# Conv taps spread over more of attention, a latent projection that starts on half its input, and two smaller moves in a decoder trunk kernel on one Trainium2 core

## The chip, the core and the metric

One core of a Trainium2 chip (trn2). The time is the device time of one execution in microseconds. A core has TensorE (PE, matrix products and transposes), VectorE (DVE), ScalarE (ACT), GpSimd (POOL), SyncE (SP, which here only issues DMA transfers), and 16 DMA engines. Each engine works its own instructions in order and waits for others by semaphores.

## What is computed

Two layers of a decoder trunk over 1024 tokens of width 1024, all in float32. Cut to what matters:

```python
for i in range(2):
    a = rmsnorm(h, mix_norm_g[i])
    z = a @ w_in[i]                       # 1024 x 1440: 512 SGU | 512 conv | 416 latent (MLA)
    z_sgu, z_conv, c_q, c_kv, k_pe = split(z)
    y_a = sgu_mixer(z_sgu, ...)
    y_b = conv_mixer(z_conv, ...)         # a * sigmoid(g), causal depthwise conv of 31 taps, layernorm, silu, 256 x 256
    y_c = mla_mixer(c_q, c_kv, k_pe, ...) # 8 heads, causal softmax attention, q and k of width 96, v of width 64
    h = h + concat(rmsnorm(y_a), rmsnorm(y_b), rmsnorm(y_c)) @ w_o[i]
    m = rmsnorm(h, ffn_norm_g[i])
    h = h + hier_moe(m, ...)              # top 2 of 32 experts
    gate = sigmoid(rmsnorm(h, ple_norm_g[i]) @ ple_gate_w[i])
    e = rmsnorm(p[i] @ ple_proj_w[i], ple_post_norm_g[i])
    h = h + gate * e
```

## The kernel before

The 1024 tokens are 8 tiles of 128 rows. `h` stays on the chip. Every engine has its own program, and all loop over the two layers. A layer has five stages, and the order of the work inside each is written by hand, as a list of (lag, function) pairs for each engine that `lag_loop` works off: an entry (2, f) handles tile t + 2 in step t, an entry (-3, f) tile t - 3. Steps before tile 0 and after tile 7 are written out, so a tile index is a plain integer there. `settle` counts up a semaphore that nobody waits for. `turned`, `turn` and the rest wait on `Steps`, which are semaphores with counted, named events.

1. **Projections.** For each tile: ScalarE squares `h`, GpSimd takes the inverse root, VectorE scales (`norm(0)`, factors in `gains[:, MIX]`), TensorE transposes 8 blocks (`turn(0)`, line 1708), ScalarE copies them out of PSUM in two halves (lines 902 and 905, events `FX.lo` and `FX.hi`: blocks 0 to 3 and 4 to 7 of the contraction), and TensorE multiplies by `w_in` in three products of 8 steps each through the helper `product` (line 1739): `z_mla` (416 columns), `z_first` and `z_glu` (512 each). One step of a float32 product is two matmul instructions in the profile, so a product is x16. In the list of TensorE, `z_mla` of tile t + 1 stands behind the transposes of the queries of tile t - 2 (`r_turn`, line 1858) and ahead of everything of tile t. Its wait for both halves is in `turned(0, t)`. The q and k of each tile are stored to DRAM and loaded back head by head by SyncE.
2. **The conv on VectorE.** `taps(t, u, some)` (lines 1218 to 1223) works 256 columns (two tiles) of one half of the channels: tap k is one multiply-add of 128x256 into one of two accumulators, and after the last of the 31 taps line 1229 joins the two. There are 8 such jobs in a layer, numbered as the tiles. In the projection stage they run with a lag of 3, cut in three parts (taps 0 to 7, 8 to 18, 19 to 30), between the other VectorE work. Job 5 falls to the steps behind tile 7, where only it, the last gated half (line 1251) and the last `sgu_out` are left. Jobs 6 and 7 are done in attention: two taps behind the other VectorE work of each block j >= 4.
3. **Attention.** Head by head, and in a head block by block (j = 0 to 7: query tile j against key tiles 0 to j). TensorE: scores of the next block (lines 1896, 1899), transposes of this one (1910), output of the last one (1926). VectorE: row maximum of the next block (1393), copy of up to four transposed blocks (1399), output scaling of the last (1404, 1406), then taps. ScalarE: exponential (1017) and the other transposed blocks (1011). The program is unrolled.
4. **Output product, router and experts.** `w_o` product (`w_half`), `norm_m` with the factors in `gains[:, FFN]`, router, expert blocks. An expert block of 64 rows leaves its result in `y_half`, which is `gains[:, FFN, 0:512]`. The stage of the experts streams weights from DRAM.
5. **Gate.** For each tile VectorE adds the expert results (lines 1652, 1655), `norm(2)` scales by `ple_norm_g` (in `gains[:, MIX]`), TensorE transposes (`turn(2)`) and multiplies by the gate weights in two halves of 8 steps (`ple_main`: g_lo, g_hi), ScalarE takes the tanh of each half, VectorE gates and adds. The list of TensorE is (1, transposes), (0, both halves). The next layer's `mix_norm_g` overwrites `gains[:, MIX]`, so SyncE loads it behind all of the gate stage's norms.

## Time and profile before

| what | us |
|---|---|
| median of 3 runs (lowest, highest) | 2265.92 (2262.76, 2273.8) |
| the profiled execution, whole | 2260.44 |
| its span | 2258.3 |
| busy: TensorE, VectorE, ScalarE, GpSimd | 2032.6 (90%), 1097.2 (49%), 576.5 (26%), 377.6 (17%) |

The span runs from the first to the last recorded instruction; the whole is 2.1 us longer. Layer 0 fills about the first half of the span, layer 1 the second: the projections run from 0 to 281 us and from 1146 to 1408 us, attention behind them to 471 and 1598 us. A row of a timeline gives the start in us, the duration in us, the engine and line, the operation with its tiles and shape, how many instructions are merged (x), and in brackets the idle time in front of it on that engine with what ended it.

### The profile page before, as it was taken

To read this page: it belongs to the slowest core of one execution; us is meant where nothing else is said; L and a number is where in the kernel's file an instruction comes from. 1 tells how busy PE (TensorE), PEld (TensorE's weight loads), DVE (VectorE), ACT (ScalarE), POOL (GpSimd) and SP (SyncE) were. 2 spreads that over 40 slices of the span, in tenths; PEclk is the share of its full clock that TensorE was granted. 3 is DMA by queue.
4 is the path that set the end of the run, shared out by engine and by line. 5 is a ranking of instruction groups with operands and counts; after the bars stand their busy time and mean duration, and the time that the engine had idled before them with its cause. 6 is when DMAs were issued, how large, how long until landed. Compare 5 with 4: busy or idle time off the path is not lost.

```text
span 2258.3 us, 34453 instructions
## 1 busy us (share of the span) xinstructions
PE 2032.6 (90%) x8968; PEld 1167.5 (52%) x8968; DVE 1097.2 (49%) x2503; ACT 576.5 (26%) x1329; POOL 377.6 (17%) x550
## 2 busy tenths in 40 slices
PE   4999789999979999968979997999999799999698
PEld 2555467755545444434435554777555454444344
DVE  2479978855341111115424799788552411111353
ACT  2333234322131111111123332344221311111111
POOL 1222200012012222210012222000120122222100
PEclk9999889999989999988989998899999899999799
DMA  6011141000179999955310111410002799999422
GB/s 242 15 28 28 40 151 43 15 10 29 70 296 363 382 381 380 381 222 212 113 28 15 28 28 50 141 43 15 10 28 82 290 374 388 382 377 382 169 84 93
DMA packets 122170, 361.93 MB, mean 160 GB/s; under 512 B 18805, under 2 KB 53957, under 8 KB 105172
## 3 DMA queue, kind: packets, MB, share of 16 engines
q1 hardware_dynamic: 104980, 318.74, 38.6%
q0 software_dynamic: 14784, 33.59, 3.9%
q10 hardware_dynamic: 2304, 8.39, 1.0%
q8 instruction: 46, 0.75, 0.1%
q14 instruction: 56, 0.46, 0.1%
HBM read 319.50 MB, written 59.51 MB: 168 GB/s over the span
## 4 chain that ended last, share of the span: by engine, by line
PE 65%; DMA 15%; DVE 8%; issue 8%; ACT 1%; SPq 1%; POOLq 1%; POOL 1%; DVEq 0%; ACTq 0%
PE ps L1739 33%; DMA region_a<-moe_inputs,idx_ring 8%; PE ps L1896 5%; PE ps L2096 4%; PE ps L1926 4%; DMA region_c<-in_moe_w_up_dram 3%; PE ps L2075 3%; PE ps L1708 3%; PE ps L1910 2%; PE ps L2071 2%; PE ps L1828 2%; DMA region_a<-in_moe_w_up_dram 2%; PE ps L2056 2%; DMA h<-in_x_dram 1%; PE ps L1996 1%
## 5 line engine op out<-in xcount | busy, mean ns | idle before, releaser
L1739 PE MATMUL ps<-region_b,region_c 128*128 128x512 f32 x1024 | 452.8, 598 | 2.7 <-DVE region_c L1202 2.7
L1739 PE MATMUL ps<-region_a,region_c 128*128 128x512 f32 (+1 forms) x768 | 320.9, 572 | 14.9 <-ACT region_c L905 14.9
L1739 PEld LDWEIGHTS ps<-region_b,region_c 128*128 128x128 f32 x1024 | 194.0, 192 | 229.6 <-issue 229.1
L1739 PEld LDWEIGHTS ps<-region_a,region_c 128*128 128x128 f32 x768 | 145.4, 192 | 172.9 <-issue 172.9
L1619 DVE SCALAR_TENSOR_TENSOR region_a<-region_a,ps 128x128 f32<-128x128 f32 x66 | 23.4, 355 | 368.6 <-ACT region_a L1080 364.7
L1896 PE MATMUL ps<-region_c 96*128 96x512 f32 (+3 forms) x384 | 157.9, 522 | 0.0
L2075 PE MATMUL ps<-region_c,region_a 128*128 128x512 f32 x336 | 148.3, 594 | 8.2 <-DMA region_c<-in_moe_w_up_dram 8.1
L1926 PE MATMUL ps<-region_c,region_a 128*128 128x64 f32 x1152 | 148.0, 275 | 0.0
L1926 PEld LDWEIGHTS ps<-region_c,region_a 128*128 128x128 f32 x1152 | 144.5, 198 | 0.0
L1708 PE MATMUL ps<-ident,region_c 128*128 128x128 f32 x496 | 71.1, 293 | 77.1 <-DVE region_c L1186 59.6
L1017 ACT ACTIVATE region_a<-ps,neg_max 128x128 f32<-128x128 f32 (+7 forms) x128 | 94.9, 741 | 126.7 <-DVE neg_max L1393 125.2
L1393 DVE TENSOR_REDUCE neg_max<-ps 128x1 f32<-128x128 f32 (+7 forms) x128 | 96.5, 755 | 43.0 <-PE ps L1899 42.3
L1708 PEld LDWEIGHTS ps<-ident,region_c 128*128 128x128 f32 x496 | 62.6, 151 | 102.5 <-DVE region_c L1186 74.0
L1080 ACT ACTIVATE region_a<-ps 128x128 f32<-128x128 f32 x66 | 21.8, 331 | 346.1 <-PE ps L2075 233.2
L1910 PE MATMUL ps<-ident,region_a 128*128 128x128 f32 x576 | 88.3, 281 | 22.1 <-ACT region_a L1017 22.1
L2075 PEld LDWEIGHTS ps<-region_c,region_a 128*128 128x128 f32 x336 | 62.2, 190 | 86.5 <-issue 86.5
L2056 PE MATMUL ps<-ident,region_a 128*128 128x128 f32 (+1 forms) x528 | 59.6, 256 | 38.8 <-DMA region_a<-moe_inputs,idx_ring 19.6
L1910 PEld LDWEIGHTS ps<-ident,region_a 128*128 128x128 f32 x576 | 63.2, 144 | 52.2 <-ACT region_a L1017 35.2
L2071 PE MATMUL ps<-region_c,region_a 128*64 128x256 f32 x736 | 88.2, 394 | 1.3 <-DVE region_a L1613 1.2
L2075 PE MATMUL ps<-region_a 128*128 128x512 f32 x192 | 84.7, 594 | 4.0 <-DMA region_a<-in_moe_w_up_dram 2.7
L2056 PEld LDWEIGHTS ps<-ident,region_a 128*128 128x128 f32 (+1 forms) x528 | 47.9, 142 | 77.4 <-issue 77.4
L1896 PEld LDWEIGHTS ps<-region_c 96*128 96x128 f32 x384 | 66.6, 200 | 32.2 <-issue 31.7
(341 smaller groups left out, 2955.0 us busy)
## 6 DMA issues: line engine op xcount, KB each, us to landing
region_c<-in_moe_w_gate_dram SPq DMA_DIRECT2D x44, 1024.0 KB
region_c<-in_moe_w_up_dram SPq DMA_DIRECT2D x44, 1024.0 KB
region_c<-in_moe_w_down_dram SPq DMA_DIRECT2D x44, 1024.0 KB
region_a<-in_moe_w_gate_dram SPq DMA_DIRECT2D x22, 1024.0 KB
region_a<-in_moe_w_up_dram SPq DMA_DIRECT2D x22, 1024.0 KB
region_a<-in_moe_w_down_dram SPq DMA_DIRECT2D x22, 1024.0 KB
region_c<-choice_outputs SPq DMA_DIRECT2D x32, 512.0 KB, 4.4
qk_heads<-gains SPq DMA_DIRECT2D x32, 384.0 KB, 4.2
```

The costliest lines, as they stand in the source:

```text
L1017: nc.scalar.activation(prob[j % 2][:, 0:n], banks(2 * (j % 2))[:, 0:n], ACT.Exp, bias=neg_max[:, j % 2:j % 2 + 1], accum_out=denom[:, j:j ...
L1393: v.tensor_reduce(neg_max[:, j % 2:j % 2 + 1], banks(2 * (j % 2))[:, 0:(j + 1) * P], AX.X, ALU.max, negate=True).then_inc(*X_max.next(f"ma ...
L1708: ins = T(bank(b + k // 4, P * (k % 4), P * (k % 4) + P), src[:, P * k:P * k + P], ident[:, :])
L1739: ins = mm(dst, lhsT[:, k, :], w[:, k, a:b], start=(k == 0), stop=(k == KD - 1))
L1828: ins = mm(bank(half, 0, w), cnT[:, k, :], w_uq[:, k, w * half:w * half + w], start=(k == 0), stop=(k == 1))
L1896: mm(bank(b + c // 512, 0, w), q, k_ring[u][0:QK, c:c + w], start=True, stop=not last, skip_group_check=True)
L1910: ins = T(bank(4 + k // 4, P * (k % 4), P * (k % 4) + P), prob[j % 2][:, P * k:P * k + P], ident[:, :])
L1926: ins = mm(bank(6 + j % 2, 0, HEAD), prob_t[j % 2][:, k, :], vals[:, k, head, :], start=(k == 0), stop=(k == j))
L2056: ins = T(bank(k // 4, w * (k % 4), w * (k % 4) + w), x_blk[s][0:w, P * k:P * k + P], ident[0:w, 0:w])
L2071: ins = mm(ps[a:a + HALF, 2, 0:F].rearrange("p (a f) -> p a f", a=2), xT[:, k, 0:HALF], pair[:, :, P * c:P * c + P], start=(k == 0), stop= ...
L2075: ins = mm(bank(2).rearrange("p (a f) -> p a f", a=2), xT[:, k, :], w_gu[s][:, :, k, :], start=(k == 0), stop=(k == KD - 1))
L2096: ins = mm(bank(4 + half), hid_t[:, k, :], w_dn[s][:, k, 512 * half:512 * half + 512], start=(k == 0), stop=(k == 1))
```

## The change

Four edits.

- **Taps.** Job 5 of the conv leaves the steps behind tile 7 of the projection stage. Attention now works jobs 5, 6 and 7, 93 taps in place of 62: one tap behind the VectorE work of each block j < 4, two behind each block j >= 4, so 12 in a head, from head 0 on.
- **Latent projection.** `z_mla` no longer goes through `turned` and `product`. It waits for the first four transposed blocks, multiplies them, then waits for the other four and multiplies those. Its other waits come first.
- **Gate stage.** The list of TensorE becomes: first half of tile t, transposes of tile t + 1, second half of tile t.
- **Norm factors.** `ple_norm_g` goes to `gains[:, FFN]`, and the next layer's `mix_norm_g` is loaded to `gains[:, MIX]` right behind it, ahead of the expert weights, and not at the end of the layer. The 64-row expert results go to `junk[:, 0:512]`.

```diff
-        y_half = gains[:, FFN, 0:512]
+        y_half = junk[:, 0:512]
...
                 sp.dma_start(gains[:, BRANCH], I["ple_post_norm_g"][l].partition_broadcast(P)).then_inc(ple_loaded, 16)
-                sp.dma_start(gains[:, MIX], I["ple_norm_g"][l].partition_broadcast(P)).then_inc(ple_loaded, 16)
+                sp.wait_ge(*FM.a.before(TILES * l + TILES))
+                settle(sp, passed)
+                sp.dma_start(gains[:, FFN], I["ple_norm_g"][l].partition_broadcast(P)).then_inc(ple_loaded, 16)
+
+                def next_mix():
+                    load_mix((l + 1).with_bounds(max_val=DEPTH - 1))
+
+                guarded(sp, l < DEPTH - 1, next_mix)
...
-                def next_mix():
-                    sp.wait_ge(*FX.a.before(24 * l + 24))
-                    settle(sp, passed)
-                    load_mix((l + 1).with_bounds(max_val=DEPTH - 1))
-
-                guarded(sp, l < DEPTH - 1, next_mix)
...
-                                                         gains[:, BRANCH if ph == 1 else MIX, a:b], ALU.mult, ALU.mult)
+                                                         gains[:, (MIX, BRANCH, FFN)[ph], a:b], ALU.mult, ALU.mult)
...
-                        if not (isinstance(t, int) and t >= TILES - 2):
+                        if not (isinstance(t, int) and t >= TILES - 3):
                             taps(t, u, range(a, b))
...
-                    if j >= 4:
-
-                        some = range(8 * (hd % 4) + 2 * (j - 4), min(8 * (hd % 4) + 2 * (j - 4) + 2, TAPS))
-                        taps(TILES - 2 + hd // 4, hd // 4, some, acc_last)
+                    first = 12 * hd + j + max(j - 4, 0)
+                    for k in range(first, min(first + 1 + (j >= 4), 3 * TAPS)):
+                        taps(TILES - 3 + k // TAPS, (1 + k // TAPS) % 2, [k % TAPS], acc_last)
...
                 def z_mla(t, u, i):
                     g = TILES * l + t
-                    turned(0, t)
                     pe.wait_ge(*ZM_act.after(g - 1))
                     pe.wait_ge(w_in_loaded[2], 16 * l + 16)
-                    product(bank(4, 0, MLA_IN), aT_mix[u], w_in, 1024, IN).then_inc(*ZM_pe.next("z_mla"))
+                    settle(pe, passed)
+
+                    for steps_, some in ((FX.lo, range(0, 4)), (FX.hi, range(4, KD))):
+                        pe.wait_ge(*steps_.after(24 * l + t))
+                        settle(pe, passed)
+                        for k in some:
+                            ins = mm(bank(4, 0, MLA_IN), aT_mix[u][:, k, :], w_in[:, k, 1024:IN], start=(k == 0), stop=(k == KD - 1))
+                    ins.then_inc(*ZM_pe.next("z_mla"))
...
-                def ple_main(t, u, i):
-                    g = TILES * l + t
-                    turned(2, t)
-                    for k, half in enumerate(("g_lo", "g_hi")):
+                def ple_half(k):
+                    def go(t, u, i):
+                        g = TILES * l + t
+                        if k == 0:
+                            turned(2, t)
                         pe.wait_ge(*E_act.after(g - 1, ("t_lo", "t_hi")[k]))
-                        product(bank(2 + k), aT[u], ple_g, 512 * k, 512 * k + 512).then_inc(*E_pe.next(half))
-
-                lag_loop(pe, [(1, turn(2)), (0, ple_main)])
+                        product(bank(2 + k), aT[u], ple_g, 512 * k, 512 * k + 512).then_inc(*E_pe.next(("g_lo", "g_hi")[k]))
+                    return go
+
+                lag_loop(pe, [(0, ple_half(0)), (1, turn(2)), (0, ple_half(1))])
```

How the rows of the program move, at three places. **TensorE, in the loop of the projection stage, from the query transposes to the latent projection.** In brackets stand the semaphores that a row waits for: `x_lo` and `x_hi` are the two copied halves, `zm_act` the copy of the last latent result. Before:

```order
L1858 MATMUL ps<-ident,region_b 96x128 x7
L394 UNCONDITIONAL_BRANCH
L1734 ISA
L1753 ISA [waits x_hi,x_lo]
L1739 MATMUL ps<-region_a,region_c 128x416 [waits w_in_loaded2,zm_act]
L1739 MATMUL ps<-region_a,region_c 128x416 x7
```

Now:

```order
L1863 MATMUL ps<-ident,region_b 96x128 x7
L394 UNCONDITIONAL_BRANCH
L1751 ISA
L1756 ISA [waits zm_act,w_in_loaded2]
L1759 MATMUL ps<-region_a,region_c 128x416 [waits x_lo]
L1759 MATMUL ps<-region_a,region_c 128x416 x3
L1759 MATMUL ps<-region_a,region_c 128x416 [waits x_hi]
L1759 MATMUL ps<-region_a,region_c 128x416 x3
```

The wait for the second half has moved from two rows ahead of the product into its middle, and the first matmul itself now waits for the first half alone.

**VectorE, from the last join of the projection stage into head 0 of attention.** Before:

```order
L1229 TENSOR_TENSOR conv_in<-region_b,region_c 128x256
L1392 ISA
L1393 TENSOR_REDUCE neg_max<-ps 128x1
L1392 REGISTER_ALU
L1393 TENSOR_REDUCE neg_max<-ps 128x1
L1398 ISA
L1399 COPY region_a<-ps 128x128
L1392 REGISTER_ALU
L1393 TENSOR_REDUCE neg_max<-ps 128x1
```

Now:

```order
L1309 TENSOR_TENSOR region_c<-region_b 128x256
L1392 ISA
L1393 TENSOR_REDUCE neg_max<-ps 128x1
L1392 REGISTER_ALU
L1393 TENSOR_REDUCE neg_max<-ps 128x1
L1398 ISA
L1399 COPY region_a<-ps 128x128
L1216 ISA
L1217 ISA
L1218 TENSOR_SCALAR region_b<-conv_in,conv_w_cols 128x256
L1392 REGISTER_ALU
L1393 TENSOR_REDUCE neg_max<-ps 128x1
```

The first row maximum follows `sgu_out` at once, the 31 taps and the join in front of it are gone, and the first of them stands between the second and the third row maximum.

**TensorE, the loop of the gate stage.** Before:

```order
L1708 MATMUL ps<-ident,region_c 128x128 x8
L1734 ISA
L2128 ISA
L1739 MATMUL ps<-region_b,region_c 128x512 x8
L2128 REGISTER_ALU
L1739 MATMUL ps<-region_b,region_c 128x512 x8
```

Now:

```order
L2134 ISA
L1738 MATMUL ps<-region_b,region_c 128x512 x8
L1714 ISA
L1720 REGISTER_ALU
L1707 MATMUL ps<-ident,region_c 128x128 x8
L2134 REGISTER_ALU
L1738 MATMUL ps<-region_b,region_c 128x512 x8
```

The eight transposes have gone from ahead of the first half to between the halves; the number of instructions is the same.

## Rows read from the trace of the kernel before

**Rows 1.** Busy us (x) of PE, PEld, DVE, ACT, POOL, clock: projections.

```profile
189.50:218.20 28.70, 27.95 (x99) 15.33 (x98) 25.88 (x65) 9.82 (x25) 7.60 (x6) 1.00 0.11 27
...
274.00:288.00 14.00, 5.89 (x25) 4.52 (x25) 13.68 (x36) 3.00 (x7) 0.00 (x0) 0.62 0.29 73
```

**Rows 2.** The same columns, attention of layer 0.

```profile
330.00:372.00 42.00, 41.67 (x285) 32.67 (x284) 32.79 (x82) 16.53 (x40) 0.00 (x0) 1.00 0.15 41
...
394.50:417.00 22.50, 21.57 (x148) 16.95 (x146) 19.49 (x52) 8.85 (x22) 1.29 (x2) 1.00 0.12 32
```

**Rows 3.** VectorE timeline, end of the projections.

```profile
273.48 0.42 DVE L1251 SCALAR_TENSOR_TENSOR region_b<-region_b,ps 128x256 f32<-128x256 f32 x1
...
286.28 0.48 DVE L1223 SCALAR_TENSOR_TENSOR region_b<-conv_in,conv_w_cols,region_b 128x256 f32<-128x256 f32 x1
286.79 0.42 DVE L1229 TENSOR_TENSOR conv_in<-region_b,region_c 128x256 f32<-128x256 f32 x1
287.13 0.61 DVE L1393 TENSOR_REDUCE neg_max<-ps 128x1 f32<-128x128 f32 x2
```

**Rows 4.** TensorE timeline, the same place.

```profile
273.95 0.69 PE L1794 MATMUL ps<-ident,region_b 128*128 128x128 f32 x2 [4.15 <-DVE region_b L1251]
...
280.74 0.30 PE L1899 MATMUL ps<-mask_b,ident_b 128*128 128x128 bf16 x1
287.96 0.48 PE L1910 MATMUL ps<-ident,region_a 128*128 128x128 f32 x1 [6.92 <-ACT region_a L1017]
```

**Rows 5.** SyncE timeline, loads of heads 0 and 1.

```profile
285.96 2.67 SPq L565 DMA_DIRECT2D region_c<-qk_heads  x6
```

**Rows 6.** TensorE timeline, block 5 of head 0; blocks 0, 5 of head 2.

```profile
298.01 1.51 PE L1896 MATMUL ps<-region_c 96*128 96x512 f32 x4
...
332.51 0.28 PE L1910 MATMUL ps<-ident,region_a 128*128 128x128 f32 x1
...
339.67 1.51 PE L1896 MATMUL ps<-region_c 96*128 96x512 f32 x4
```

**Rows 7.** VectorE timeline, head 2, row maxima of blocks 2, 3.

```profile
335.32 0.56 DVE L1393 TENSOR_REDUCE neg_max<-ps 128x1 f32<-128x384 f32 x1 [0.27 <-PE ps L1899]
...
336.69 0.69 DVE L1393 TENSOR_REDUCE neg_max<-ps 128x1 f32<-128x512 f32 x1
```

**Rows 8.** ScalarE timeline, head 2, exponential of block 3.

```profile
337.42 0.69 ACT L1017 ACTIVATE region_a<-ps,neg_max 128x512 f32<-128x512 f32 x1 [0.83 <-DVE neg_max L1393]
```

**Rows 9.** TensorE timeline, head 2, transposes of block 3.

```profile
338.61 0.60 PE L1910 MATMUL ps<-ident,region_a 128*128 128x128 f32 x4
```

**Rows 10.** TensorE waits, attention of layer 0 (total us, times, longest).

```profile
PE ps L1910 <- ACT region_a L1017: 11.0, 12, 6.9
```

**Rows 11.** TensorE timeline, latent projections of tile 5 (layer 0), 1 (layer 1).

```profile
153.87 5.82 PE L1739 MATMUL ps<-region_a,region_c 128*128 128x416 f32 x16 [0.76 <-ACT region_c L905]
...
1168.75 5.83 PE L1739 MATMUL ps<-region_a,region_c 128*128 128x416 f32 x16 [2.19 <-ACT region_c L905]
```

**Rows 12.** ScalarE timeline, ahead of the first of these.

```profile
152.44 0.59 ACT L902 COPY region_c<-ps 128x512 f32<-128x512 f32 x1 [5.92 <-PE ps L1739]
152.92 0.59 ACT L905 COPY region_c<-ps 128x512 f32<-128x512 f32 x1
```

**Rows 13.** TensorE timeline, behind the first two latent projections of layer 0.

```profile
45.72 4.36 PE L1828 MATMUL ps<-region_b 128*128 128x384 f32 x8 [7.49 <-ACT region_b L966]
```

**Rows 14.** VectorE timeline, GELU of tiles 4 and 5, layer 0.

```profile
173.80 0.69 DVE L1241 SCALAR_TENSOR_TENSOR region_b<-region_b,ps 128x512 f32<-128x512 f32 x1 [0.44 <-ACT region_b L915]
...
202.43 0.69 DVE L1241 SCALAR_TENSOR_TENSOR region_b<-region_b,ps 128x512 f32<-128x512 f32 x1 [0.83 <-ACT region_b L915]
```

**Rows 15.** TensorE timeline, start of the gate stage, layer 0.

```profile
1025.42 1.96 PE L1708 MATMUL ps<-ident,region_c 128*128 128x128 f32 x8 [5.03 <-DVE region_c L1202]
```

**Rows 16.** SyncE timeline, load of the next norm factors.

```profile
1120.34 0.33 SPq L501 DMA_DIRECT2D gains<-in_mix_norm_g_dram  x1
```

**Rows 17.** VectorE timeline, first norm of layer 1.

```profile
1153.92 1.28 DVE L1186 SCALAR_TENSOR_TENSOR region_c<-h,rstd,gains 128x1024 f32<-128x1024 f32 x1 [5.13 <-issue]
```

## Prediction

> **What bounds the kernel now.** I first cut the span into its stages by the engines' busy times. In the full tiles of the projection stage TensorE is busy 27.95 of 28.7 us and VectorE 25.88; in the last stretch before attention TensorE has 5.89 of 14 us and VectorE 13.68, with a granted clock of 0.62 [rows 1]. So the stage starts bound by TensorE, with VectorE close behind, and ends bound by VectorE. In attention it is TensorE again: 41.67 of 42 us, against VectorE's 32.79, and in the heads that also carry the back end of the conv 21.57 against 19.49 of 22.5 [rows 2]. Then I went to the timelines at the places that the diff touches, to see which wait ends last there.
>
> **Taps, the end of the projection stage.** VectorE does the last gated half at 273.48. Then come the 31 taps of job 5 up to 286.28, the join at 286.79, and the first row maximum at 287.13 [rows 3]. TensorE turned that gated half at 273.95, had the scores of blocks 0 and 1 written at 281.05 (280.74 + 0.31), and then sat 6.92 us until the first transposes at 287.96 [rows 4]. With job 5 gone VectorE waits for the scores, not the reverse. Its row maximum comes at about 280.0, the exponential ends near 280.8, and the transposes follow the scores of block 1 at about 281.05. **Gain 6.9 us a layer**, which is all of the idle time, not the 12.8 us that VectorE loses in work: 31 x 0.40 (the taps start 0.40 apart) + 0.42.
>
> What is late next is TensorE's own run of transposes and scores. The loads behind it have room: those of heads 0 and 1 are issued from 285.96 on [rows 5], and only blocks 6 and 7 of head 0 need the late ones. Block 5's scores start at 298.01 [rows 6], so block 6 comes some 15 us behind the issue now and some 7 behind it after.
>
> **The clock there.** At 298.01 TensorE starts on block 5 of head 0, 10.05 us after the first transposes. In head 2, at full clock, the same stretch takes 339.67 - 332.51 = 7.16 us [rows 4, 6]. The difference, 2.9 us, is what the low of the two clock levels (1.2 and 2.4 GHz) costs here. Now TensorE works from 273.95 to 281.05 with short gaps, idles 6.92, and works on. Without the idle time it will be at the high level sooner. The bounds are 0 (the low clock lasts as much of head 0 as before) and 2.9; I take the middle, **1.5 a layer**, since no row shows this stretch without the pause.
>
> **Taps, in attention.** Each head now carries 12 taps, where it had 8 on its larger blocks: 4 more, 1.6 us of VectorE. Lower bound 0, upper bound all of it, 31 taps and a join, 12.8 a layer. Nearest rows: in head 2 VectorE is idle 0.27 ahead of the row maximum of block 2 and has no idle time ahead of block 3's [rows 7]. With a tap (0.40) in both places block 3's maximum comes 0.40 + 0.13 late at most. Its exponential ends at 338.11, and TensorE takes the transposes at 338.61 [rows 8, 9], so 0.50 of that is covered. All TensorE's waits for exponentials in this attention stage are 11.0 us in 12 cases, of which 6.9 is the pause above; the other eleven share 4.1 [rows 10]. I take 0.1 us a head: **loss 0.8 a layer**. If VectorE's cover were gone, the price would be the upper bound.
>
> **Latent projection.** TensorE waits 0.76 us for the second copied half before this product [rows 11]. The first half is ready at 153.03, the second at 153.51, and the product starts 0.36 behind that [rows 12]; the rows of the program ahead of it are waits. Now the first matmul waits for the first half alone, and the other waits stand in front. It should start at 153.15, so 0.7 earlier. The four steps on the first half take half of 5.82, 2.9 us, and the second half is ready 0.48 behind the first, so the wait inside costs nothing. In layer 0 the products of tiles 0 and 1 buy nothing, as TensorE idles 7.49 us behind them, for input that is still loading [rows 13]. That leaves 6 x 0.7 = 4.2, or **4.0** as tile 2 is a little tighter. In layer 1 all eight count. Tile 1's wait is 2.19 [rows 11], but most of it ends with the first half, so 0.7 there too: 8 x 0.7, **5.5**.
>
> VectorE must follow. It idles 0.44 and 0.83 us for the GELU of tiles 4 and 5 [rows 14], and similar for 3 and 6. It carries no taps before tile 3's step, so up to there it shifts with TensorE; from there it can give up 0.44 + 0.83 + about 0.8 = 2.1 us for three more products of 0.7. It just does. Bounds for this edit: 0, and the whole waits: 12 of 0.76 and two larger ones in layer 1, some 12 us.
>
> A rule speaks against such a split. The Trainium skill ("TensorE: Matmul & The Clock Gate", section "HAM oscillation — how this bites in real kernels") advises to run all contraction steps of a tile before waiting, so that TensorE stays warm. By that rule a pause inside the product could send it to the low clock. The rows say there is no pause, and I keep the gain.
>
> **Gate stage.** TensorE starts its second set of transposes at 1025.42, 5.03 us late, released by VectorE's copy of tile 0 [rows 15]. The first half product waits for the same copy, so it now starts at that moment, and the transposes follow it. The sum of the work up to the last product is the same. Behind the first tile the products follow without a gap. **0.**
>
> **Norm factors.** The load of `mix_norm_g` is issued at 1120.34 [rows 16] and VectorE's first norm of layer 1 runs at 1153.92 behind 5.13 us in which the trace names no engine that held it [rows 17]. The load was issued 33 us before that. The earlier load adds 0.5 MB while SyncE waits for the router's result anyway, and the added wait for the `m` norms has been met before SyncE gets there, since it stored those same tiles. The small result goes to another buffer of the same kind. **0.**
>
> **The sum.** Layer 0: 6.9 + 1.5 - 0.8 + 4.0 = 11.6. Layer 1: 6.9 + 1.5 - 0.8 + 5.5 = 13.1. Together 24.7 us. The profiled execution took 2260.44 and would take 2235.7. The median of the three runs is 5.5 us above it, so I expect a median of **2241**.
>
> **Rivals.**
> - *VectorE sets the pace of the projections.* Against TensorE's new 28.0 us a tile it has 25.88 of work and its waits on ScalarE inside a tile. If those leave no room, the split's 9.5 us are gone and the end of the stage keeps its gain: 2265.9 - 15.2 = 2250.7.
> - *Head 0 waits for something else.* The late loads or the last stores, or a clock that stays low, take the place of the pause. Then 2 x (6.9 + 1.5) goes and only the split stays, less the attention's loss: 2265.9 - 9.5 + 1.6 = 2258.
> - *VectorE becomes the bound in attention, and the projections too.* Each moved tap then delays a row maximum, an exponential and the transposes behind it. Price 12.8 a layer against 6.9 saved, 11.8 in all, with nothing from clock or split: 2277.7. It decides once 1.6 us a head no longer fits. Against it: VectorE idles 42 - 32.79 us in two plain heads, 3.0 in one with the conv's back end [rows 2].
> - *The split drops the clock.* If TensorE did pause at the wait inside the product, and ran the last four steps at the low level, they would take up to 2.9 us longer in each of the 16 products. Half of that, 23 us, gives 2241 + 23 = 2264. No row shows a pause there, since 0.48 fits into 2.9 [rows 11, 12]. The rule of the page named above is this mechanism.
> - *The change doesn't do what it says* for two of its four edits; that is in the sum already.
>
> **Chances.** The forecast 0.70. VectorE's pace in the projections 0.14. Another wait in head 0, 0.09. The clock in the split 0.02. VectorE bound in attention 0.05. A measurement can tell about 0.5%, 11.3 us, from no change, so faster means under 2254.6: the first two cases and a little of the third, 0.85. Same 0.10, slower 0.05. The range: below 2241 lie the clock's full 2.9 a layer, an attention that loses nothing, and the 0.76 in place of 0.7, together 5.5, and the same again for the spread of a median of three; above it the first rival and 5 us for that spread. 2230 to 2256.
>
> **What would show it.** The gap of 6.92 ahead of the first transposes of attention gone, the row maxima held by TensorE's scores. The latent projections led by under 0.2 us of idle time behind line 902. Tiles of the projection stage 27.9 to 28.0 us apart. Heads no more than 0.3 longer. The gate stage and the start of layer 1 unchanged in length. I am wrong if VectorE shows no idle time ahead of line 1241, or TensorE's waits in attention grow by more than 3 us.

## The result, and the profile after

| | before | after |
|---|---|---|
| median of four runs each (lowest, highest), us | 2264.34 (2262.33, 2273.8) | 2235.89 (2234.3, 2236.8) |
| ratio after / before, 95% interval | | 0.986 (0.984 to 0.988) |
| the profiled execution, us | 2260.44 | 2236.55 |
| its span, us | 2258.3 | 2234.4 |

The change makes the kernel faster by 28.4 us by the medians and by 23.9 by the two profiled executions; the forecast was 24.7 for the profiled execution and a median of 2241. A second set of runs of both gave medians of 2236.04 (2231.29 to 2237.92) and 2264.78. The work is the same: TensorE is busy for 2028.5 us, where it was 2032.6.

```profile
PE 2028.5 (91%) x8968; PEld 1162.2 (52%) x8968; DVE 1093.6 (49%) x2503; ACT 576.6 (26%) x1329; POOL 377.2 (17%) x550
```

**Stages.** Windows of the trace of the changed kernel (busy us and instruction count of PE, PEld, DVE, ACT, POOL; clock; DMA), to be held against [rows 1, 2]: one full tile of the projections, the stretch from the last gated half to the first row maximum, two plain heads, one head with the conv's back end.

```profile
188.20:216.10 27.90, 27.85 (x98) 15.27 (x97) 26.18 (x66) 9.72 (x24) 7.32 (x6) 1.00 0.11 28
272.50:278.60 6.10, 4.90 (x22) 4.23 (x23) 0.73 (x3) 1.93 (x4) 0.00 (x0) 0.50 0.00 0
317.30:359.30 42.00, 41.38 (x282) 32.36 (x281) 35.51 (x91) 16.52 (x40) 0.00 (x0) 1.00 0.14 38
382.30:404.80 22.50, 21.55 (x146) 16.93 (x146) 20.70 (x55) 8.98 (x22) 1.29 (x2) 1.00 0.11 32
```

A tile of the projections takes 27.9 us and TensorE has 27.85 of work in it. Ahead of the first row maximum VectorE now has 0.73 us of work in 6.1, where it had 13.68 in 14. In attention it has 35.51 us in 42 and 20.70 in 22.5.

**The end of the projections.** TensorE's timeline of layer 0, which answers to [rows 4, 6]:

```profile
272.51 0.69 PE L1799 MATMUL ps<-ident,region_b 128*128 128x128 f32 x2 [3.26 <-DVE region_b L1251]
...
279.30 0.31 PE L1904 MATMUL ps<-mask_b,ident_b 128*128 128x128 bf16 x1
279.53 0.48 PE L1915 MATMUL ps<-ident,region_a 128*128 128x128 f32 x1
279.80 1.17 PE L1901 MATMUL ps<-region_c 96*128 96x384 f32 x2
280.81 0.22 PE L1904 MATMUL ps<-mask_b,ident_b 128*128 128x128 bf16 x1
...
285.41 1.51 PE L1901 MATMUL ps<-region_c 96*128 96x512 f32 x4
```

and VectorE's, which answers to [rows 3]:

```profile
272.03 0.42 DVE L1251 SCALAR_TENSOR_TENSOR region_b<-region_b,ps 128x256 f32<-128x256 f32 x1
...
278.58 0.29 DVE L1393 TENSOR_REDUCE neg_max<-ps 128x1 f32<-128x128 f32 x1 [5.34 <-PE ps L1904]
```

The idle time of 6.92 us ahead of the first transposes is gone, and VectorE now waits 5.34 us for the scores. The second thing to see is the mask matmul: 0.31 us at 279.30, 0.22 at 280.81. It is the same instruction on the same shape, so between them the clock rose. From the first transposes to block 5 it is 5.88 us, where it was 10.05.

The granted clock over 40 us around this place, first before the change and then with it, in layer 0:

```profile
265.00:305.00 40.00, 25.30 (x117) 18.39 (x115) 32.37 (x85) 10.45 (x22) 0.00 (x0) 0.70 0.59 196
262.00:302.00 40.00, 32.91 (x199) 25.44 (x197) 29.68 (x80) 14.04 (x31) 0.89 (x1) 0.83 0.57 190
```

The mean clock is 0.70 and becomes 0.83 (in layer 1 it goes from 0.66 to 0.87). As the lower of the two levels is 0.50, that is 24 us at the low level before and 14 with the change (27 and 10 in layer 1).

**The latent projection.** Tile 5 of layer 0 on ScalarE and TensorE, then tile 1 of layer 1, against [rows 11, 12]:

```profile
152.05 0.59 ACT L902 COPY region_c<-ps 128x512 f32<-128x512 f32 x1 [5.92 <-PE ps L1738]
152.53 0.59 ACT L905 COPY region_c<-ps 128x512 f32<-128x512 f32 x1
...
152.78 5.83 PE L1759 MATMUL ps<-region_a,region_c 128*128 128x416 f32 x16
...
1158.35 5.83 PE L1759 MATMUL ps<-region_a,region_c 128*128 128x416 f32 x16 [1.50 <-ACT region_c L902]
```

The product starts 0.14 us behind the end of the first copy (152.05 + 0.59), and 0.34 ahead of the end of the second. Its 16 instructions take 5.83 us, as they did (5.82), so there is no pause inside.

**The two smaller edits.** TensorE's first gate product, SyncE's load of the next norm factors and VectorE's first norm of layer 1, against [rows 15, 16, 17]:

```profile
1017.29 9.06 PE L1738 MATMUL ps<-region_b,region_c 128*128 128x512 f32 x16 [5.06 <-DVE region_c L1202]
...
610.28 0.37 SPq L501 DMA_DIRECT2D gains<-in_mix_norm_g_dram  x1
...
1146.19 1.28 DVE L1186 SCALAR_TENSOR_TENSOR region_c<-h,rstd,gains 128x1024 f32<-128x1024 f32 x1 [4.97 <-issue]
```

The wait of 5.06 us for tile 0's copy stands ahead of the first product now, where it stood ahead of the second transposes (5.03). The factors are loaded over 500 us sooner, and VectorE still idles 4.97 us ahead of that norm (5.13 before).

To see where the time went, the same landmarks were read in two profiles of each kernel (the second ones are runs y0_before and y1_change below). Values are us, layer 0 and layer 1, first profile / second profile.

| stretch | before, layer 0 | layer 1 | change, layer 0 | layer 1 |
|---|---|---|---|---|
| latent product of tile 0 to that of tile 2 | 46.57 / 48.13 | 38.09 / 40.20 | 48.88 / 48.64 | 36.02 / 36.37 |
| from there to attention's first scores | 211.22 / 211.30 | 209.82 / 211.31 | 208.77 / 206.34 | 206.32 / 208.84 |
| first scores to first transposes | 8.71 / 8.72 | 8.72 / 8.72 | 1.72 / 1.72 | 1.72 / 1.73 |
| first transposes to block 5 of head 0 | 10.05 / 7.27 | 9.84 / 10.08 | 5.88 / 5.59 | 5.58 / 5.91 |
| all of head 0 | 28.79 / 26.01 | 28.58 / 30.57 | 17.63 / 17.34 | 17.33 / 17.67 |
| head 1 to head 7, starts | 130.04 / 130.05 | 130.05 / 130.06 | 130.63 / 130.64 | 130.61 / 130.62 |
| head 7 to the first output product | 33.82 / 33.52 | 33.82 / 32.21 | 32.62 / 33.45 | 33.43 / 32.57 |
| output product, router, experts, to the gate's first transposes | 546.52 / 545.72 | 528.08 / 529.09 | 551.57 / 548.46 | 529.81 / 532.01 |
| from there to the next latent product, or the end | 139.76 / 140.44 | 131.68 / 131.31 | 139.15 / 139.81 | 131.47 / 131.30 |

("All of head 0" holds the two rows above it; what runs ahead of the first latent product is not in the table.) By the means of the two profiles and both layers together: head 0 gave 22.0 us, of which 14.0 is the pause; the stretch from tile 2's latent product to the first scores 6.7; the stretch from tile 0's to tile 2's 1.5. What is left (the start, the way from head 7 to the output product, the gate stage) gave 2.5 together. Attention's heads 1 to 6 took 1.15, and the experts' stretch took 6.2 back. That comes to 25.3, which is the difference of the mean spans (2259.85 and 2234.5).

### The profile page after: what moved, and what is told of

Read it like the earlier page. It is cut to its first block, busy times and chain, and to the rows that moved or that the text cites. A ratio compares the mean times of both kernels' runs of the same rounds, so it can differ in the third digit from the quotient of the medians.

```text
span 2234.4 us, 34473 instructions
## 1 busy us (share of the span) xinstructions
PE 2028.5 (91%) x8968; PEld 1162.2 (52%) x8968; DVE 1093.6 (49%) x2503; ACT 576.6 (26%) x1329; POOL 377.2 (17%) x550
## 4 chain that ended last, share of the span: by engine, by line
PE 64%; DMA 16%; DVE 9%; issue 8%; ACT 1%; POOLq 1%; POOL 1%; SPq 1%; DVEq 0%; ACTq 0%
PE ps L1738 30%; DMA region_a<-moe_inputs,idx_ring 11%; PE ps L2101 5%; PE ps L1901 4%; PE ps L1759 4%; PE ps L1931 4%; PE ps L1707 2%; PE ps L2080 2%; PE ps L1915 2%; PE ps L1833 2%; PE ps L2061 2%; DMA region_c<-in_moe_w_up_dram 2%; DMA h<-in_x_dram 1%; DVE neg_max L1393 1%; PE ps L2076 1%
## 5 line engine op out<-in xcount | busy, mean ns | idle before, releaser
L1738 PE MATMUL ps<-region_a,region_c 128*128 128x512 f32 x512 | 225.1, 594 | 0.0
L1738 PEld LDWEIGHTS ps<-region_a,region_c 128*128 128x128 f32 x512 | 96.8, 191 | 117.7 <-issue 117.7
L1901 PE MATMUL ps<-region_c 96*128 96x512 f32 (+3 forms) x384 | 152.7, 507 | 0.0
L1707 PE MATMUL ps<-ident,region_c 128*128 128x128 f32 x496 | 69.2, 288 | 66.6 <-DVE region_c L1186 59.2
L1759 PE MATMUL ps<-region_a,region_c 128*128 128x416 f32 x256 | 96.1, 529 | 3.8 <-ACT region_c L902 3.0
```

The source lines that it names most:

```text
L1707: ins = T(bank(b + k // 4, P * (k % 4), P * (k % 4) + P), src[:, P * k:P * k + P], ident[:, :])
L1738: ins = mm(dst, lhsT[:, k, :], w[:, k, a:b], start=(k == 0), stop=(k == KD - 1))
L1759: ins = mm(bank(4, 0, MLA_IN), aT_mix[u][:, k, :], w_in[:, k, 1024:IN], start=(k == 0), stop=(k == KD - 1))
L1901: mm(bank(b + c // 512, 0, w), q, k_ring[u][0:QK, c:c + w], start=True, stop=not last, skip_group_check=True)
```

## The experiments

Ten edited kernels ran, and the two kernels themselves once more. "The change" is the changed kernel, and the diffs are against it. x5, x6, x7 and y0 have one run each.

### The change without its taps edit (x1_no_taps)

```diff
-                        if not (isinstance(t, int) and t >= TILES - 3):
+                        if not (isinstance(t, int) and t >= TILES - 2):
...
-                    first = 12 * hd + j + max(j - 4, 0)
-                    for k in range(first, min(first + 1 + (j >= 4), 3 * TAPS)):
-                        taps(TILES - 3 + k // TAPS, (1 + k // TAPS) % 2, [k % TAPS], acc_last)
+                    if j >= 4:
+                        some = range(8 * (hd % 4) + 2 * (j - 4), min(8 * (hd % 4) + 2 * (j - 4) + 2, TAPS))
+                        taps(TILES - 2 + hd // 4, hd // 4, some, acc_last)
```

> The change with its taps edit taken back: job 5 again behind tile 7 of the projection stage, attention with 62 taps. Theory A (the pause is worth its idle time and a stretch at the low clock): in each layer the idle time of about 7 us ahead of the first transposes of attention is back, and the stretch from them to the scores of block 5 of head 0 takes about 10 us again in place of 5.9. That is some 11 us a layer, 2 x 11.2 = 22 us over the change's 2236, so about 2258. Theory B (the clock gain came from elsewhere, for instance from the split): only the pause is back, 2 x 7 = 14, about 2250, with the stretch at 6 to 7 us. Theory C (attention pays for its extra taps with 1 us or more a layer): the attention stage behind head 0 is shorter than in the change by that much, and the time comes out under 2256.

Measured: 2253.57 (2247.42 to 2259.55, ten runs), 0.995 of the kernel before (0.993 to 0.997). The pause is back in both layers, and from it to block 5 TensorE's timeline of layer 0 reads:

```profile
284.62 0.48 PE L1916 MATMUL ps<-ident,region_a 128*128 128x128 f32 x1 [6.91 <-ACT region_a L1017]
...
291.59 1.51 PE L1902 MATMUL ps<-region_c 96*128 96x512 f32 x4
```

The pause is 6.91 and 6.92 us, but the stretch behind it took 6.97 and 7.28 us, not the 10 of theory A: that is the size that theory B gave. Still it is 1 to 2 us more than in most layers without the pause (5.6 to 6.2), and TensorE is at the low clock until 3.6 and 4.3 us behind the first transposes. In the changed kernel it is at the high level within 1.1 us of them. So the pause costs clock as well, by an amount that differs from one execution to the next (the kernel before has 10.05, 9.84, 7.27 and 10.08 in its two profiles). Heads 1 to 6 took 130.05 and 130.04, so theory C's 1 us a layer is too much: the price of the 31 extra taps there is 0.6 a layer. The pause alone is 14.0 us of what the edit is worth. The medians can't give the rest closely, as they come from different sets of runs: the kernel before had 2267.14 beside x1 and x2, and 2264.34 beside the change. x1 lies 13.6 under the first and the change 28.4 under the second, which makes the edit worth 15 us; the bare difference of the two medians is 17.7, and the ratios (0.995 and 0.986) give 20.

### The change without the split (x2_no_split)

```diff
-                    pe.wait_ge(*ZM_act.after(g - 1))
-                    pe.wait_ge(w_in_loaded[2], 16 * l + 16)
-                    settle(pe, passed)
-
-                    for steps_, some in ((FX.lo, range(0, 4)), (FX.hi, range(4, KD))):
-                        pe.wait_ge(*steps_.after(24 * l + t))
-                        settle(pe, passed)
-                        for k in some:
-                            ins = mm(bank(4, 0, MLA_IN), aT_mix[u][:, k, :], w_in[:, k, 1024:IN], start=(k == 0), stop=(k == KD - 1))
-                    ins.then_inc(*ZM_pe.next("z_mla"))
+                    turned(0, t)
+                    pe.wait_ge(*ZM_act.after(g - 1))
+                    pe.wait_ge(w_in_loaded[2], 16 * l + 16)
+                    product(bank(4, 0, MLA_IN), aT_mix[u], w_in, 1024, IN).then_inc(*ZM_pe.next("z_mla"))
```

> The change with its latent projection taken back to one wait for both halves and eight steps in one go. Theory A: tiles of the projection stage are 28.6 us apart in place of 27.93, in both layers, and the time is 4 to 5 us longer in layer 0 and 5.6 in layer 1: about 2246. Theory B (VectorE's taps behind tile 7 set the end of the stage whatever the products do): the tiles are 28.6 apart but the end of the stage moves by less than half of it: about 2240. In the start of layer 0 the first query products should again run at the high clock (4.36 us for the x16 group, 5.49 in the change) if the split is what lowers it there.

Measured: 2251.59 (2244.94 to 2260.15, ten runs), 0.994 of the kernel before (0.992 to 0.996); its profiled execution took 2247.8. Tiles are 28.63 apart again. From tile 2's latent product to attention's first scores it took 211.30 and 209.85 us. That is 2.5 to 5.0 more than the change's in layer 0 and 1.0 to 3.5 more in layer 1. From tile 0's to tile 2's it took 38.10 in layer 1, 1.7 to 2.1 more. By the profiled executions the split is worth 11 us, of which these stretches show about 8; another 4 is a late clock at the start of attention in layer 1 (below), which is not the split's. Theory A's 4 to 5 us stand in layer 0; in layer 1 the mean is 4.2 of its 5.6. Theory B fails, as the end of the stage moves by most of it. The medians are 15.7 us apart; against the kernel before of its own set x2 gains 15.6 us, which makes the split worth 13, and the ratios give 17. Taps and split together are then worth 28, 33 or 37 us, by set, by bare difference or by ratio, where all four edits gave 28.4. So each of these figures holds to some us only, and the stretches of the profiles are the better guide.

The first query products of layer 0 took 4.66 us here, against 5.49 in the change. But they took 4.35 in x1 and 4.37 in x5, which have the split, and 5.48 in the second profile of the kernel before, which has not. So the split is not what lowers the clock there.

This run has no pause in layer 1, and yet the clock came late. TensorE's first transposes, the mask matmul of block 4, and the scores of block 5:

```profile
1398.29 0.48 PE L1909 MATMUL ps<-ident,region_a 128*128 128x128 f32 x1
...
1406.23 0.31 PE L1898 MATMUL ps<-mask_b,ident_b 128*128 128x128 bf16 x1
...
1408.20 1.51 PE L1895 MATMUL ps<-region_c 96*128 96x512 f32 x4
```

The stretch took 9.91 us, as long as it did behind the pause.

### The change without the gate stage's order (x3_no_gate), and without the move of the norm factors (x4_no_norm)

```diff
-                def ple_half(k):
-                    def go(t, u, i):
-                        g = TILES * l + t
-                        if k == 0:
-                            turned(2, t)
-                        pe.wait_ge(*E_act.after(g - 1, ("t_lo", "t_hi")[k]))
-                        product(bank(2 + k), aT[u], ple_g, 512 * k, 512 * k + 512).then_inc(*E_pe.next(("g_lo", "g_hi")[k]))
-                    return go
-
-                lag_loop(pe, [(0, ple_half(0)), (1, turn(2)), (0, ple_half(1))])
+                def ple_main(t, u, i):
+                    g = TILES * l + t
+                    turned(2, t)
+                    for k, half in enumerate(("g_lo", "g_hi")):
                         pe.wait_ge(*E_act.after(g - 1, ("t_lo", "t_hi")[k]))
+                        product(bank(2 + k), aT[u], ple_g, 512 * k, 512 * k + 512).then_inc(*E_pe.next(half))
+
+                lag_loop(pe, [(1, turn(2)), (0, ple_main)])
```

> The change with the gate stage's old order: transposes of tile t + 1, then both halves of tile t. Theory A: nothing, since the first half waited for the same copy: 2236 within 1.5 us. Theory B (the transposes no longer fill the wait for the tanh of the last tile, or the first products now run at the low clock): the gate stage is up to 2 us a layer longer or shorter, 2232 to 2240.

x4 takes back the five pieces of the diff that name `y_half`, `ple_norm_g` and `next_mix`.

> The change with the norm factors back in their old places: one buffer for both, the next layer's factors loaded behind the gate stage's norms. Theory A: nothing, 2236 within 1.5 us. Theory B (the earlier 0.5 MB load and the added wait are what cost the change some 3 us between the gather and the last expert product of layer 0, 325.8 us against 322.8 before): that stretch is 323 again and the time about 2233.

Measured: 2232.51 (2229.75 to 2238.66) for x3, 2238.63 (2237.86 to 2241.42) for x4, four runs each. The stretch from the gate's first transposes on took 139.32 and 132.68 us in x3, 139.61 and 132.07 in x4, against 139.15 / 139.81 and 131.47 / 131.30 in the change: in layer 0 both lie between the change's two values, in layer 1 both are up to 1.4 us longer. Neither edit of the change lengthened it. The experts' stretch took 547.3 and 530.4 in x4. From the first transposes of gathered rows to the last expert product of layer 0 it took 323.3, which is the length that theory B named (323.1 before, 326.3 in the first profile of the change). But kernels that keep the moved load took 321.8 (c2) and 322.3 (x3) there and up to 328.3 (c3), and x4's median is 2238.6 and not 2233. So one profile at 323 is no sign of that edit. x4 also had the late clock, in layer 0. Windows over its first 12 us of attention, and over the first 8 of the change's; the column behind POOL is the clock:

```profile
275.00:279.00 4.00, 4.00 (x15) 2.55 (x15) 1.80 (x6) 1.93 (x5) 0.00 (x0) 0.50 0.35 83
279.00:283.00 4.00, 4.00 (x13) 2.55 (x13) 2.61 (x10) 1.45 (x4) 0.00 (x0) 0.50 0.53 147
283.00:287.00 4.00, 4.00 (x16) 2.92 (x15) 2.19 (x6) 0.89 (x2) 0.00 (x0) 0.58 0.97 244
```

```profile
278.00:282.00 4.00, 4.00 (x17) 2.42 (x16) 2.25 (x7) 2.27 (x6) 0.00 (x0) 0.69 0.36 86
282.00:286.00 4.00, 4.00 (x26) 2.89 (x25) 3.83 (x11) 1.70 (x5) 0.00 (x0) 1.00 0.55 148
```

TensorE was busy all of both. In one it stayed at 0.50, the lower level, for 8 us and more; in the other it rose in the first window (0.69 is a mean of the two levels).

### Sixteen taps in a head (x5_taps16)

```diff
-                    first = 12 * hd + j + max(j - 4, 0)
-                    for k in range(first, min(first + 1 + (j >= 4), 3 * TAPS)):
+                    first = 16 * hd + 2 * j
+                    for k in range(first, min(first + 2, 3 * TAPS)):
```

> The change with two taps in every block of attention, 16 in a head in place of 12, so that the 93 taps are done by block 6 of head 5. In the change heads 1 to 7 take 130.6 us in all against 130.05 with the 62 taps of the kernel before, so 31 taps more cost 0.6. Theory A (TensorE sets the pace and VectorE has room; the 0.3 of head 2 is one tap on its path): 4 taps more a head, 1.6 us of VectorE, cost 0.1 to 0.4 in each of the heads 1 and 2, up to 1 us in heads 3 and 4, which carry the conv's back end, and give nothing back in 6 and 7, which lose theirs: 1 to 3 us a layer in all. Theory B (VectorE is at its limit with 12): each of the heads 1 to 4 is 1 to 1.6 us longer, 4 to 8 us a layer.

Measured: heads 1 to 5 took 21.56, 21.43, 21.56, 23.02 and 23.67 us in layer 0 (in the change 20.85, 21.12, 20.85, 22.07, 22.88), head 6 22.21 (22.86). So four taps more cost 0.7, 0.3, 0.7, 1.0 and 0.8, and their absence gives 0.65 back: 2.8 a layer in all, the same in layer 1. TensorE's waits for exponentials over attention of layer 0, in the change and here:

```profile
PE ps L1915 <- ACT region_a L1017: 4.5, 12, 0.9
```

```profile
PE ps L1915 <- ACT region_a L1017: 5.2, 15, 0.7
```

Theory A's sum holds, at its upper end, though head 1 pays more than its 0.4 and head 6 gives something back. VectorE's room is used up between 12 and 16: the step from 8 to 12 cost 0.1 a head on average, the step from 12 to 16 cost 0.7. Both steps put one tap more behind each of the blocks 0 to 3, so it is the room there that is meant. In head 1 VectorE is busy 18.86 of 21.56 us, but its timeline shows no idle time from 299.21 up to the row maximum of block 7 at 313.22; in the change it shows some ahead of the row maxima of blocks 5 and 6 as well (0.26 and 0.27). The whole took 2240.72 (one run). The waits above are only 0.7 us more in all, but the trace lists TensorE's weight loads apart, and their waits for exponentials go from 12.0 us in 21 cases to 15.3 in 28. Those 3.3 us are near the 2.8.

### The waits' order without the split (x6_waits)

```diff
-                    for steps_, some in ((FX.lo, range(0, 4)), (FX.hi, range(4, KD))):
-                        pe.wait_ge(*steps_.after(24 * l + t))
-                        settle(pe, passed)
-                        for k in some:
-                            ins = mm(bank(4, 0, MLA_IN), aT_mix[u][:, k, :], w_in[:, k, 1024:IN], start=(k == 0), stop=(k == KD - 1))
-                    ins.then_inc(*ZM_pe.next("z_mla"))
+                    turned(0, t)
+                    settle(pe, passed)
+                    product(bank(4, 0, MLA_IN), aT_mix[u], w_in, 1024, IN).then_inc(*ZM_pe.next("z_mla"))
```

> The change with the latent projection in one piece, all eight steps behind the wait for both halves, but with the waits for the last latent result and the weights in front as in the change. It tells the split from the order of the waits. Theory A (the split itself is worth the 0.48 us that lie between the two halves, the rest of the 0.70 a tile is the shorter way from the wait to the first matmul): tiles 28.4 us apart, against 27.93 in the change and 28.63 before. Theory B (all of it is the split): 28.6. Theory C (all of it is the order): 27.9.

```profile
153.33 5.82 PE L1738 MATMUL ps<-region_a,region_c 128*128 128x416 f32 x16 [0.50 <-ACT region_c L905]
```

Measured: tiles 28.36 us apart in both layers. The wait is 0.50 where it was 0.76. So of the 0.70 a tile 0.26 comes from the order of the waits and 0.44 from the split: theory A. The whole took 2253.81 in one run; the rest of that is the clock (9.95 us at the start of attention in layer 0, a latent product of 7.52 us in layer 1, tile 1) and an experts' stretch of 549.7 and 533.7.

### Two candidates (c1_defer, c2_defer2)

After the change TensorE still waits 3.26 us for the last gated half of the projections, behind the last 12 taps of job 4, and VectorE then idles 5.34 us. The first candidate puts those taps into that idle time:

```diff
+                def conv_end(t, u, i):
+                    if isinstance(t, int):
+                        return
+                    guarded(v, True if u else i < 2, lambda: taps(t, u, range(19, TAPS)))
...
-                             ... (0, gate_scale), (-3, conv(19, TAPS))])
+                             ... (0, gate_scale), (-3, conv_end)])
+                CT_vec.at = 19
+                taps(TILES - 4, 0, range(19, TAPS))
```

> A candidate: the change, and the last 12 taps of job 4 moved from the end of tile 7's step to behind the last sgu_out, where VectorE idles 5.3 us ahead of the first row maximum. The gated half of tile 7 is then made at about 267.0 and not at 272.0 (times of layer 0 of the change). Theory A (TensorE's 3.26 us of waiting for it is what the end of the stage is made of): the first scores come 3.3 us sooner in each layer, the deferred 12 x 0.40 + 0.42 = 5.2 us of taps still end before or near the first row maximum, and the time is 6 to 6.5 us under the change's, about 2230. Theory B (the deferred taps now hold the first row maximum, as job 5 did before): part of it is given back as idle time ahead of the first transposes, 2 to 3 us a layer, about 2234. Theory C (with less waiting the granted clock rises sooner as well): 1 to 4 us more a layer, about 2226.

Measured: 2230.23 (2228.19 to 2236.41, four runs), 0.985 of the kernel before (0.982 to 0.987). VectorE's gated half, the join of job 4 and the first row maximum, then TensorE's transposes of the gated half:

```profile
265.11 0.42 DVE L1256 SCALAR_TENSOR_TENSOR region_b<-region_b,ps 128x256 f32<-128x256 f32 x1 [0.27 <-issue]
...
273.06 0.43 DVE L1229 TENSOR_TENSOR region_c<-region_b,region_c 128x256 f32<-128x256 f32 x1
274.13 0.29 DVE L1400 TENSOR_REDUCE neg_max<-ps 128x1 f32<-128x128 f32 x1 [0.64 <-PE ps L1911]
```

```profile
267.15 0.63 PE L1806 MATMUL ps<-ident,region_b 128*128 128x128 f32 x2
```

The taps end ahead of the scores, and TensorE doesn't wait for the gated half. From tile 2's latent product to the first scores it takes 205.18 and 203.53 us; the change's best was 206.32. That is 2.8 us a layer when the clock falls alike, theory A. Part of the wait that went (3.26 and 4.15 us in the two layers) comes back as a longer one for ScalarE further on (line 1000: 2.15 and 3.86 us, where it was 1.19). c1's profile also shows the late clock in layer 1: 9.85 us from the first transposes to block 5.

The second candidate also moves the last 12 taps of job 3, from step 6 to behind the gated half in step 7:

```diff
-                lag_loop(v, [(-1, gelu_glu), (2, norm(0)), ...
+                def conv_end_3(t, u, i):
+                    if u and not isinstance(t, int):
+                        CT_vec.at = 19
+                        guarded(v, i > 0, lambda: taps(t, u, range(19, TAPS)))
+
+                lag_loop(v, [(-1, gelu_glu), (-4, conv_end_3), (2, norm(0)), ...
...
-                    guarded(v, True if u else i < 2, lambda: taps(t, u, range(19, TAPS)))
+                    guarded(v, i < 1 if u else i < 2, lambda: taps(t, u, range(19, TAPS)))
```

> The candidate before, and the last 12 taps of job 3 as well moved behind the gated half of tile 6, one step on. VectorE makes that gated half at about 238.6 and not at 243.9, so TensorE's wait of 3.06 us for it goes. Theory A (VectorE, which has 5.2 us more to do in the step of tile 7, had idle time of 2.5 us there, and starts it 5 us sooner in relation to TensorE): 2 to 3 us a layer on top of the first candidate, about 2225. Theory B (VectorE sets the pace in tile 7's step, so the wait moves behind z_first): nothing on top, within 1 us a layer.

Measured: 2243.74 (2243.34 to 2245.97), 13.5 slower than the first candidate. VectorE at the start of the second, third and fourth pass of its loop over two tiles, and at the GELU of tile 7; TensorE's wait in that tile; and the instruction queue of the first candidate and of this one (packets, MB, share):

```profile
103.44 0.42 DVE L1261 SCALAR_TENSOR_TENSOR region_b<-region_b,ps 128x256 f32<-128x256 f32 x1 [4.04 <-issue]
...
165.00 0.42 DVE L1261 SCALAR_TENSOR_TENSOR region_b<-region_b,ps 128x256 f32<-128x256 f32 x1 [4.20 <-issue]
...
225.94 0.42 DVE L1261 SCALAR_TENSOR_TENSOR region_b<-region_b,ps 128x256 f32<-128x256 f32 x1 [5.10 <-issue]
...
263.97 0.68 DVE L1251 SCALAR_TENSOR_TENSOR region_b<-region_b,ps 128x512 f32<-128x512 f32 x1
```

```profile
274.53 1.94 PE L1803 MATMUL ps<-region_b,sgu_w_t 128*128 128x64 f32 x8 [5.27 <-DVE region_b L1274]
```

```profile
q14 instruction: 58, 0.48, 0.1%
```

```profile
q14 instruction: 88, 0.72, 0.1%
```

The wait behaves as in theory B, but the loss is in neither theory. VectorE has no idle time ahead of the GELU of tile 7, and TensorE waits 5.27 us behind it. And at the start of each later pass VectorE stands still for 4 to 5 us that the profile puts down to no engine; in the change these are 0.6 us at most. The tile at 153.27 takes 29.98 us in place of 27.93, 2.0 more in each layer. Most of the rest stands between tile 7's latent product and the first scores, which take 70.3 and 70.4 us, 4.7 and 6.5 more than in the first candidate. Both the third gap and the moved taps fall there, and the runs don't part them. The instruction queue moved 88 packets and 0.72 MB, where the first candidate's moved 58 and 0.48. That looks like code that no longer stays in the engine from one pass to the next, though it was not shown. The Trainium skill ("Runtime: NRT & Kernel Launch", section "Instruction fetch mechanics") says that a taken branch to a place outside of what the engine holds has to wait for a load of that code. These gaps agree with it, and the loop of the change, which also jumps back, shows none of that length.

### A block that never runs (x7_dead)

```diff
+                def dead(t, u, i):
+                    if u and not isinstance(t, int):
+                        CT_vec.at = 19
+                        guarded(v, i > 7, lambda: taps(t, u, range(19, TAPS)))
...
-                lag_loop(v, [(-1, gelu_glu), (2, norm(0)), ...
+                lag_loop(v, [(-1, gelu_glu), (-4, dead), (2, norm(0)), ...
```

> The first candidate with a second copy of the 12 taps and their join in the loop's body of VectorE's program, behind a condition that is never true, so that it never runs. In the second candidate VectorE stood still for 4.0 to 5.1 us at the start of each later pass through the loop of two tiles (99.4, 160.8 and 220.8 us in layer 0), for nothing that the profile names, and the packets of the instruction queue q14 rose from 58 to 88. Theory A (the loop's body has grown past what the engine keeps of its program, so that each jump back waits for a load of code): the same three gaps of 4 to 5 us in each layer and some 88 packets on that queue, with no tap moved. Theory B (the gaps came from the moved taps, or from passing over the block): no gap above 1 us at the start of a pass, or one elsewhere, and about 58 packets; time as the first candidate, 2230 within 6.

Measured: 2228.72 (one run), no gap above 0.62 us, 58 packets. By the text on record that is theory B. But the experiment missed: the loop has four passes, so i never exceeds 3, and 58 packets are what the first candidate has. The second copy of the taps was in all likelihood not in the program at all. It is a second look at that candidate, and the length of the loop's body as the cause of c2's gaps was not tested. It stays the likeliest reading, and open.

### Once more before and after, and the candidate with the old gate order (y0_before, y1_change, c3_defer_gate)

No edit in the first two. The third is c1_defer with x3's diff.

> The kernel before once more, for its profile. The question is whether the stretch from the first output product to the first transposes of the gate stage (output product, router and experts) differs between the kernels or from one execution to the next: it took 546.5 and 528.1 us in the two layers in the first profile of the kernel before, 551.6 and 529.8 in that of the change, and 547.3 to 550.9 and 528.6 to 533.7 in the runs with parts of it. Theory A (it wanders by 2 to 3 us by itself, since the weight transfers set its pace): here it comes out somewhere else, 545 to 550 and 527 to 532, and the stretch from the first transposes of attention to the scores of block 5 of head 0 may differ from the 10.05 and 9.84 us of the first profile. Theory B (the change costs 2 to 4 us there): again 546.5 and 528 within 0.5.

> The change once more. Theory A (wandering): the experts' stretch of layer 0 is not 551.6 but 547 to 550, and the stretch at the start of attention's head 0 is 5.6 us in one execution and up to 9.9 in another, by where the clock rises; the median stays at 2236 within 2. Theory B (the change costs 5 us in the experts' stretch of layer 0): 551 to 552 again.

> The first candidate (the change with the last 12 taps of job 4 behind the last sgu_out) with the gate stage's old order. Theory A (the gate stage's order is worth nothing, and the lower time of the run without it was the wandering of the experts' stretch): as the first candidate, 2230 within 2. Theory B (the old order is 3 us better): 2227, with the stretch from the gate's first transposes to the next layer's first latent product, or to the end of the span, shorter by 1.5 in each layer than in the first candidate.

Measured: y0 2263.52 (one run), y1 2236.04, c3 2230.09 (2220.26 to 2238.67), 0.983 of the kernel before (0.981 to 0.986). c3's stretches behind the gate's first transposes are 139.67 and 132.44, c1's 139.25 and 132.65: theory A, the gate order is worth nothing that these runs can tell. The low median of x3 was not its edit. On the experts' stretch both theories are half right. It wanders (548.46 and 532.01 in y1, where it was 551.57 and 529.81), but in the two profiles of the kernel before it is 545.7 to 546.5 and 528.1 to 529.1, and in the twelve profiles with the change or most of it 549.1 and 531.1 on average (545.6 to 553.9, 528.6 to 533.7). That is some 2.5 to 3 us a layer given back, and no one edit taken away brings them home. But four readings stand against twenty-four that spread by 8 and 5 us, so that the change costs anything there is likely and not shown.

## Why the prediction was right

It said 2241 within 2230 to 2256, faster; the median is 2235.9. By its own terms:

- **The pause, 6.9 a layer: right.** The first transposes come 1.72 behind the first scores in place of 8.71, 7.0 us in each layer, in each run that has the edit (1.85 in c2). VectorE was idle where it was said to be. The late loads did not matter: TensorE has no idle time ahead of the scores of blocks 6 and 7.
- **The clock, 1.5 a layer: right mechanism, wrong bound, and a size that differs from one execution to the next.** The upper bound of 2.9 came from the same stretch in head 2, 7.16 us. That stretch also holds the output matmuls of the head ahead of it, which head 0 has not; the shortest seen in head 0 is 5.6, so the bound should have been 4.5. In the six layers of three profiles with the pause (before twice, x1), head 0 takes 25.7 to 30.6, on average 27.6. In the fourteen layers of seven profiles without it (the change twice, x2 to x6) it takes 17.3 to 17.9 eleven times and 21.7 three times, on average 18.4. The difference of 9.2 is the pause and 2.2 for the clock. In the two profiles of the change, against the two of the kernel before, the clock gave 4. The granted clock shows the mechanism: with the pause it is back at the high level 3.6 to 13.6 us behind the first transposes, without it at the first transposes or up to 1.2 us behind them, but for the three late cases.
- **Attention's extra taps, 0.8 a layer lost: right**, 0.58 in heads 1 to 6. Half of it is in head 2 (20.83 to 21.12).
- **The split, 4.0 and 5.5: right where the clock is alike.** The period falls from 28.63 to 27.93, 0.70 as predicted, and between the products of tiles 2 and 7 that makes 5 x 0.70 = 3.5 in each layer. In layer 0 the query products start at 45.7 to 46.7 us in every profile, with the split or without, as they wait for their input; what tiles 0 and 1 gain is lost there, as said. From that start to tile 7's latent product it takes 165.4 us before and 161.4 in x1, whose query products run at the same clock (4.36 and 4.35): 4.0, the forecast. In the table the stretch from tile 0 to tile 2 is longer with the change, but mainly because tile 0's product starts sooner (20.16, where it was 21.46) and because TensorE's query products, in the first profiles, ran for 5.49 us against 4.36 before [rows 13]:

```profile
45.65 5.49 PE L1833 MATMUL ps<-region_b 128*128 128x384 f32 x8 [8.98 <-ACT region_b L966]
```

  The second profile of the kernel before has 5.48 too. In layer 1 the stretch from tile 0 to tile 2 gave 2.1 in the first profiles (38.09 to 36.02): 0.69 at tile 1 (its wait went from 2.19 to 1.50) and 0.44 at tile 2, and 0.93 from the clock, as tile 0's product took 6.57 us in place of 7.50. Without that 0.93 it is 1.1 + 3.5 = 4.6, and tile 0's own wait of 0.95, which lies ahead of the stretch, makes 5.6. From tile 7's product to the first scores nothing of it is lost where the clock is alike: 66.7 us occurs in both kernels, and 68.2 in the kernel before and in x1, x3 and x5, which have the split. The changed kernel's other value, 69.2, goes with a low clock of 6.8 us on the way, where the 68.2 goes with 3.4.
- **VectorE must follow: it just does.** Against 0.44 and 0.83 before [rows 14], its idle time ahead of the GELU of tiles 4 and 5 is none and 0.18:

```profile
172.88 0.68 DVE L1241 SCALAR_TENSOR_TENSOR region_b<-region_b,ps 128x512 f32<-128x512 f32 x1
...
200.63 0.69 DVE L1241 SCALAR_TENSOR_TENSOR region_b<-region_b,ps 128x512 f32<-128x512 f32 x1 [0.18 <-ACT region_b L915]
```

  The forecast named no idle time at this line as a sign of being wrong. At tile 4 it came true in both layers, yet the tiles stay 27.93 apart, so the sign was set too sharply. The rival "VectorE sets the pace of the projections" missed by a few tenths of a microsecond a tile, and c2 shows something like it when the 12 taps land in tile 7's step.
- **Gate stage and norm factors, 0: right**, within what the profiles can tell.
- **The step that was missing** is the stretch of the experts. I had no term for it, and in the two profiles of each kernel it gave back 3.1 us a layer on average. Windows of the changed kernel there (the last two columns are DMA's busy share and GB/s):

```profile
700.00:750.00 50.00, 46.73 (x244) 24.71 (x239) 9.50 (x21) 8.53 (x22) 12.25 (x21) 1.00 1.01 387
800.00:850.00 50.00, 45.51 (x211) 23.61 (x212) 9.08 (x20) 7.95 (x20) 12.66 (x21) 1.00 0.99 372
```

  DMA is busy throughout, TensorE is not, and the rate it reaches differs from window to window. What lengthens the stretch stays open; the two suspects in the change (the 0.5 MB ahead of the weights, and where the 64-row results go) were taken back in x4, and the stretch was no shorter than in some that keep them.
- **From the profile to the median.** I added to the forecast the 5.5 us by which the median before lay above its profiled execution. The change's profiled execution is 0.7 above its median instead. So the miss of 5 us is that addition and not the sum: 2235.7 was forecast for the profiled execution, which took 2236.55. With its fourth run the kernel before has a median only 3.9 above that execution.
- **Luck.** That the sum came within 1 us is luck. By the means of the two profiles head 0 gave 22.0 us where 16.8 were forecast, the experts took back 6.2 where nothing was, and the split's stretches gave 8.2 for 9.5. In other terms: the clock gave 5 us more than the middle of its bounds, and a stretch without a term took that much away.

The rule of the Trainium skill ("TensorE: Matmul & The Clock Gate", section "HAM oscillation — how this bites in real kernels"), to run all contraction steps before waiting, did not speak here. At the split there is no pause and the product takes its 5.83 us. The runs that had the low clock for long at the start of attention had it with the split (x4, c1) and without it (x2, x6).
